# Moving ScalarE's weight splits around two norms, spreading eight constant fills over VectorE's projections, and placing a norm's total one quarter unit later

## The reference, cut to what matters

```python
def rms_norm(x, g):
    y = xf * lax.rsqrt(jnp.mean(xf * xf, axis=-1, keepdims=True) + EPS)
    return (y * g.astype(jnp.float32)).astype(x.dtype)

# first block
x = x + 0.5 * swiglu(rms_norm(x, ffn1_norm), ...)
h = rms_norm(x, mix_norm)                         # first norm of this study
fq, fk, fv, f_logit, sq, sk, sv, g_fox, g_sb = split_columns(h @ w_in)
fq = rms_norm(fq.reshape(b, s_len, 8, 64), q_norm)   # per head
fk = rms_norm(fk.reshape(b, s_len, 8, 64), k_norm)
log_f = jax.nn.log_sigmoid(f_logit + forget_bias)
y_fox = forgetting_attention(fq, fk, fv, log_f)   # q.k/8 + F_t - F_s, causal softmax
...
x = x + swiglu(...); x = x + sigmoid(rms_norm(x, ple_norm) @ w_ple_gate) * (p @ w_ple_proj)

# second block
h = rms_norm_2(x, g_norm)                         # second norm of this study
hy_in, z_hy, c_q, c_kv, k_rope, z_attn, gate_hy, gate_attn = jnp.split(h @ w_in_2, split_at)
k_spec = hyena_filter_spectra(...)                # rfft of filters, does not depend on x
```

## Time and profile before

| | |
|---|---|
| median of 3 runs | 1712.06 us (1712.02 to 1712.94) |
| profiled execution | 1712.45 us, of which 1710.3 us are the span from the first to the last instruction |
| TensorE busy | 1694.5 us, 99% of the span |
| VectorE, GpSimd, ScalarE busy | 1035.8, 716.5, 642.6 us |
| TensorE clock granted | 1.000 of full speed over the whole span |

### The profile page before, as it was taken

One profiled execution on the slowest core, in us unless ns is written; L12 is line 12 of the kernel. 1 busy time (PEld: TensorE's weight loads), 2 busy tenths in 40 slices (PEclk: granted clock), 3 DMA queues, 4 the chain that ended last, 5 costly groups with the idle time before them and its releaser, 6 DMA issues.

```text
span 1710.3 us, 21166 instructions
## 1 busy us (share of the span) xinstructions
PE 1694.5 (99%) x7666; PEld 1384.3 (81%) x7666; DVE 1035.8 (61%) x1224; ACT 642.6 (38%) x899; POOL 716.5 (42%) x303
## 2 busy tenths in 40 slices
PE   9999999999999999999999999999999999999999
PEld 7887888887788888888888888888777778888887
DVE  6766577428565456357664567785644753869441
ACT  5222322235565756321322322213446644333321
POOL 2444344433434431344444444444455434444443
PEclk9999999999999999999999999999999999999999
DMA  5333232325221221243423232323342014332243
GB/s 194 99 108 103 73 97 93 112 83 190 78 66 60 97 64 36 79 134 95 139 98 112 85 99 95 109 99 105 111 140 70 26 47 163 99 98 94 92 145 113
DMA packets 42815, 171.04 MB, mean 100 GB/s; under 512 B 4937, under 2 KB 5065, under 8 KB 41452
## 3 DMA queue, kind: packets, MB, share of 16 engines
q1 hardware_dynamic: 38736, 148.13, 26.6%
q10 hardware_dynamic: 3996, 21.73, 3.6%
HBM read 159.22 MB, written 10.62 MB: 99 GB/s over the span
## 4 chain that ended last, share of the span: by engine, by line
issue 50%; PE 34%; POOL 14%; POOLq 1%; ACT 0%; DMA 0%; DVE 0%; SPq 0%; ACTq 0%; DVEq 0%
POOL wlo L272 14%; PE psum L306 9%; PE psum L308 9%; PE psum L307 9%; PE psum L1723 2%; PE psum L1712 1%; PE psum L747 0%; PE psum L732 0%; POOLq L280 0%; PE psum L1684 0%; PE psum L718 0%; DMA xT<-x_dram 0%; PE psum L947 0%; PE psum L719 0%; PE psum L2416 0%
## 5 line engine op out<-in xcount | busy, mean ns | idle before, releaser
L272 POOL TENSOR_TENSOR wlo<-raw,whi 128x1024 fp32r<-128x1024 f32 (+2 forms) x258 | 664.2, 2575 | 905.2 <-ACT whi L294 904.6
L294 ACT ACTIVATE whi<-raw 128x1024 fp32r<-128x1024 f32 (+2 forms) x259 | 286.1, 1105 | 706.0 <-PE psum L308 696.1
L306 PE MATMUL psum<-h_hi,whi 128*128 128x512 f32 x1360 | 538.5, 396 | 6.9 <-POOL wlo L272 6.2
L308 PE MATMUL psum<-h_hi,wlo 128*128 128x512 f32 x1360 | 529.7, 390 | 0.0
L307 PE MATMUL psum<-h_lo,whi 128*128 128x512 f32 x1360 | 529.6, 389 | 0.0
L306 PEld LDWEIGHTS psum<-h_hi,whi 128*128 128x128 f32 x1360 | 255.4, 188 | 67.7 <-POOL wlo L272 8.9
L307 PEld LDWEIGHTS psum<-h_lo,whi 128*128 128x128 f32 x1360 | 255.5, 188 | 54.4 <-issue 3.1
L308 PEld LDWEIGHTS psum<-h_hi,wlo 128*128 128x128 f32 x1360 | 255.3, 188 | 53.5
L306 PE MATMUL psum<-mid_hi,whi 128*128 128x512 f32 x352 | 137.2, 390 | 0.0
L308 PE MATMUL psum<-mid_hi,wlo 128*128 128x512 f32 x352 | 137.0, 389 | 0.0
L307 PE MATMUL psum<-mid_lo,whi 128*128 128x512 f32 x352 | 136.9, 389 | 0.0
(11 more groups left out here) (383 smaller groups left out, 2427.9 us busy)
## 6 DMA issues: line engine op xcount, KB each, us to landing
raw<-wk_dram SPq DMA_DIRECT2D x220, 512.0 KB, 3.5
raw<-wd_dram SPq DMA_DIRECT2D x32, 704.0 KB, 4.1
raw<-wp_dram SPq DMA_DIRECT2D x8, 640.0 KB, 3.8
x_scratch<-xT ACTq DMA_DIRECT2D x2, 2048.0 KB, 7.6
spectra_scratch<-spec_out ACTq DMA_DIRECT2D x4, 1024.0 KB, 4.6
xT<-x_scratch ACTq DMA_DIRECT2D x8, 512.0 KB, 4.3
spec<-spectra_scratch ACTq DMA_DIRECT2D x2, 2048.0 KB, 10.5
xT<-x_dram SPq DMA_DIRECT2D x4, 512.0 KB, 7.7
```

Source lines behind the costliest of these rows:

```text
L272: pool.tensor_tensor(wlo[s][:, 0:w], raw[s][:, 0:w], whi[s][:, 0:w].bitcast(F32), ALU.subtract).then_inc(lo_ready, 1)
L294: act.activation(whi[s][:, 0:w], raw[s][:, 0:w], ACT.Copy).then_inc(hi_ready, 1)
L306: pe.matmul(dst, s_hi, m_hi, start=start and i == 0, stop=False, **kw)
L308: last = pe.matmul(dst, s_lo, m_hi, start=False, stop=stop and i == n - 1, **kw)
```

## The change

Three edits. First, in `Norm.scalar` the split of unit `after + 1` moves from behind the last tile to behind tile 5, ahead of the copy of the second spectra unit's third quarter; this applies to both norms. Second, the eight constant fills of `fq_hi` leave the head of VectorE's fox list; each becomes the last instruction of one of the eight steps i, in a function of its own. Third, TensorE takes three quarters of the second norm's first spectra unit ahead of the norm's total, where it took two.

```diff
@@ Norm.scalar
                     elif k == 5:
+                        split_hi_to(act, after + 2)
                         filters.scalar_copy(act, o, 1, 2)
-                split_hi_to(act, after + 2)
@@ FoxProjections.vector
                 dve.wait_ge(unit_done, BASE["fox_q"])
-                any_finite = constf.rearrange("p a t -> p (a t)")
-                for h in range(HEADS):
-                    rows = other[h % 2]
-                    row = vec[rows, VEC["head_row"] + h:VEC["head_row"] + h + 1]
-                    dve.tensor_scalar(fq_hi[rows, h, :], any_finite[rows, :], 0.0, row, ALU.mult,
-                                      ALU.add).then_inc(self.cleared, 1)
                 dve.tensor_scalar(small[:, 31:32], col("q_norm"), HD ** -0.5, None, ALU.mult).then_inc(self.cleared, 1)
                 for i in range(8):
                     dve.wait_ge(self.rstd, i + 1)
                     if i == 0:
-                        dve.wait_ge(self.cleared, 9)
+                        dve.wait_ge(self.cleared, 1)
...
                         dve.tensor_copy(again, whole[main[e], h, :].bitcast(F32)).then_inc(self.ready, 1)
+                    self.vector_head_row(dve, i)
                     dve.wait_ge(self.ready, 4 * i + 4)
...
+            def vector_head_row(self, dve, h):
+                rows = other[h % 2]
+                row = vec[rows, VEC["head_row"] + h:VEC["head_row"] + h + 1]
+                any_finite = constf.rearrange("p a t -> p (a t)")
+                dve.tensor_scalar(fq_hi[rows, h, :], any_finite[rows, :], 0.0, row, ALU.mult,
+                                  ALU.add).then_inc(self.cleared, 1)
@@ TensorE's list
-            filters.tensor_unit(pe, 1, 0, 0, 2)
+            filters.tensor_unit(pe, 1, 0, 0, 3)
             norm_block2.tensor(pe)
-            filters.tensor_unit(pe, 1, 0, 2, 4)
+            filters.tensor_unit(pe, 1, 0, 3, 4)
```

## The result

The changed kernel takes 1720.43 us, median of 6 runs (1719.55 to 1720.93); the kernel before, on the same chip, 1712.26 us (1712.02 to 1713.06, 6 runs). The ratio is 1.0046, 95% interval [1.0036, 1.0056]: slower, by 8.2 us where 5.1 were forecast, and 1.6 us above the upper end of the range (1718.8). The profiled execution took 1720.41 us with a span of 1718.3 (before 1710.3).

The account below looks back on a forecast made before the run. TensorE, busy 99% of the span, was taken to bound the kernel. +5.3 us at bank 5 and -0.2 at the second norm made +5.1 on 1712.45, less 0.39 for the median: 1717.1 us, range 1709.8 to 1718.8.

Parts of the forecast that it names:

- the chain of holds up to bank 5: Fox stage: GpSimd holds VectorE's fills and copies, so bank 5 starts at 457.45 instead of 452.15, 5.3 us lost.
- The first gains: First block: earlier split and moved fills start q1 1.86 us sooner and q3 at 413.2, winning 1.9 us.
- Step 1's fill: It comes 0.26 us behind GpSimd's start and is held to 423.45; step 2 multiplies at 424.2, not 421.9.
- Then the lateness feeds itself: From step 3: each second copy is held for GpSimd; a step lasts 7.03 us, TensorE's unit 6.35.
- the five waits on the way: TensorE up to bank 5: about 0.45 for k2's weights, 1.0 v0's, 1.9 last square, 1.05 bank 4, 4.1 us bank 5.
- the price of TensorE's waits: In the sum: TensorE's waits counted at their length only, with 5.3 us lost at bank 5.
- The term of -0.2 us for the second norm: Second norm, split moved up: 1.86 us won at second unit, given back at fourth; 0.2 kept, bounds 0 and 0.5.
- Total one quarter later: Second norm: second spectra unit still starts at 1224.97, behind a wait of 1.8 instead of 0.25 us; worth nothing.
- Only half of the lateness: Rival, 0.14: step 1's fill gets in ahead of GpSimd, step 3's is held; bank 5 at 455.4, 1715.2 us.
- The gain stays: Rival, 0.17: fills in steps 1, 3 and 4 cost only 0.52 us each, the 1.9 us hold; 1710.0 us.
- It cancels: Rival, 0.08: a hold of one step, 2.3 us, is caught up before v0; within 1 us of 1712.

Follow-up runs that it names:

- the first four experiments: The kernel before with each of the three edits alone (1713.47, 1719.93, 1712.06 us), and the changed kernel with all eight fills behind step 7 (1712.84 us).

## Why the prediction came out as it did

The direction was right and so was the chain of holds up to bank 5; what TensorE's waits cost was not: 1717.1 forecast, 1720.4 measured. The two errors go opposite ways: the chain was worked out 1.1 us too long, and 3.9 us of lower clock were missing, so the total looks closer than its terms are.

**The first gains: right.** q1 came without a wait, f at 399.0 (399.4 worked out: the constants landed earlier, not later), q3 at 412.8 (413.2), a gain of 2.3 us against 1.9.

**Step 1's fill: right, and closer than worked out.** The margin was 0.12 us, not 0.26; the fill took 2.56 us. Leaving it out of the step (-9.0 us against the changed kernel, bank 5 at 450.2) shows that the loss there hangs on a hold at that place, and with a copy held in its place the loss stays.

**"Then the lateness feeds itself": right, its size 1.1 us too large.** The holds of steps 3 to 5 came as described. Of the five waits on the way, the last three came (1.6, 0.5 and 3.7 us where 1.9, 1.05 and 4.1 stood); v0's first matmul stood 0.96 us behind the head sum instead of 0.45, a wait of about 0.5 where 1.0 stood, and for k2's weights there was none (0.45 stood). Steps 1 to 6 multiplied 0.5 to 1.1 us earlier than worked out, 0.5 of it from step 1 on. Bank 5: +4.2 instead of +5.3.

**The step that failed: the price of TensorE's waits.** The sum took each wait at its length. After the 3.7 us at bank 5 and the 3.0 us at the fourth unit the granted clock was 0.50 and 0.57, and the matmuls behind cost 2.3 and 1.6 us more; with other matmuls in the waits this cost was gone. The term of -0.2 us for the second norm was right as a start time (-0.23 in the traces) and wrong as a price: the same edit made a 1.2 us wait into one of 3.0, and in that stage it is a loss, as the first edit alone showed (+1.4 us). 5.3 - 0.2 becomes 4.2 + 2.3 - 0.2 + 1.6 = 7.9.

The Trainium skill has the two levels in "TensorE: Matmul & The Clock Gate", Part 1: the lower one is the default, activity releases it, and when the change comes varies from run to run. The traces agree: 0.50 behind 3.71 us of idleness, and behind a wait of 1.70 us for q1 a clock of 1.000 in the kernel before but 0.55 in the one with the splits moved back.

**Total one quarter later: right.** 0.0 us alone, with a wait of 1.6 us where 1.8 was worked out.

**The rivals.** "Only half of the lateness" is what ran when step 1's fill was let through: bank 5 at 454.8 (455.4 worked out), the next hold in step 3. "The gain stays" needed three places to pass. With the fills behind the multiplications they do, and even then the second norm's wait took most of the gain back: 1711.4 us, not 1710.0. "It cancels" came in no version with step 1's hold: none caught up before v0.

**Still open** is which waits lower the clock. It fell in all five profiles with a wait of 3.7 us and in all nine with one of 3.0, and behind 2.60 and 2.72 us in the one profile each that had it. Behind 1.7 us (1.68 to 1.71), in eleven places of five profiles, it fell once. The times hint that it falls oftener: of the 27 runs of the kernel before beside the first four experiments, six took 1713.24 to 1713.67 us with a mean clock of 0.998 or 0.999, where the others stayed below 1712.9; none of these six was profiled. For how long it stays down varies too, from 3.4 to 6.8 us. Nor was it settled why f's earlier start won nothing in the median.

## What to carry to other kernels

Work added to an engine that has slack on average must go where that engine waits in the cycle. The same eight fills took 9.0 us less behind the multiplications than behind the copies (1711.4 against 1720.4 us), since at the end of a step they raced GpSimd for tenths of a microsecond. A wait of TensorE like those of 2.6 to 3.7 us here should be priced above its length, and even one of 1.7 us has a chance of it: merging two short waits into one long one can lose even if the next start comes earlier. When an early start is given back later, look at the list of the engine that gives it back for an instruction that waits for something unrelated. Here it was a store issue ahead of a split; with it moved, the early splits are worth 3.35 us (1706.7 us in all).

## What the runs showed of the hardware

GpSimd's subtraction, too, is lengthened when VectorE gets in first: 3.12 us instead of 2.41 with a fill, a subtraction and a memset around its start. And three versions whose longest TensorE wait was 1.6 us were steadier: ten runs within 0.44 us, six within 1.13 and six within 0.31, against 3.1 us over eleven runs of the kernel with step 1's fill last, which kept its wait of 3.0 us, and 2.9 over eleven of the kernel before with the stores moved, which kept three of 1.7. That the waits are the reason isn't shown: the kernel with step 1's fill ahead of the copies, with waits of 3.7 and 3.0 us, stayed within 0.63 us in five runs.
